# Hybrid encoder step: when the output GEMM's first operands, the last convolution and its edge rows are moved

## The reference

```python
u = jnp.concatenate([buf.astype(xin.dtype), cg * xin], axis=1)
y = sum(w[j] * u[:, j:j + S] for j in range(CONV_W))
return bg * y, u[:, S:]          # the two last rows of u are an output
...
y = jnp.concatenate([silu(z) * yb for yb, z in branches], axis=-1)
x = x + (y @ w_out)              # 2048 x 2048
...
y = x * rsqrt(mean(x * x) + eps) * g
```

## Time and profile before

| | us |
|---|---|
| median of 3 executions | 2401.81 |
| lowest, highest | 2400.15, 2405.1 |
| profiled execution, its own time | 2403.48 |
| its span in the trace | 2401.4 |
| PE busy | 2295.9 (96%) |
| DVE, ACT, POOL busy | 797.6, 481.9, 438.9 |

### The profile page before, as it was taken

The page is one execution under the profiler, slowest core; times in us unless marked ns, Lnnn a source line. Parts: engine busy times, 40 slices in busy tenths (PEclk is TensorE's granted clock), DMA queues, the critical chain, the costliest instruction groups (busy, mean ns, idle before and its releaser), DMA issues.

```text
span 2401.4 us, 35351 instructions
## 1 busy us (share of the span) xinstructions
PE 2295.9 (96%) x14176; PEld 2116.7 (88%) x14176; DVE 797.6 (33%) x1273; ACT 481.9 (20%) x798; POOL 438.9 (18%) x259
## 2 busy tenths in 40 slices
PE   6999999999989899999999999999899978999997
PEld 6899999999989899998999889999898976888886
DVE  7221122222121111153537361333231344343533
ACT  6111212222211111111111111111101013333431
POOL 2232221222121222222222122222121120000000
PEclk9999999999999999999999999999999988999999
DMA  5112414151431433231322223444434547465552
GB/s 213 56 58 68 182 44 168 55 174 51 161 112 56 150 125 124 107 96 53 114 71 95 84 69 117 126 125 126 99 108 163 197 139 263 155 224 185 187 194 87
DMA packets 158569, 298.90 MB, mean 124 GB/s; under 512 B 26124, under 2 KB 97932, under 8 KB 154656
## 3 DMA queue, kind: packets, MB, share of 16 engines
q1 hardware_dynamic: 150432, 281.63, 34.7%
q10 hardware_dynamic: 8064, 16.25, 2.1%
HBM read 238.55 MB, written 78.10 MB: 132 GB/s over the span
## 4 chain that ended last, share of the span: by engine, by line
PE 81%; DVE 9%; DMA 6%; issue 1%; SPq 1%; ACT 1%; DVEq 0%; POOLq 0%
PE G L820 18%; PE G L822 17%; PE G L821 17%; PE X L1161 3%; PE X L1160 3%; PE X L1159 3%; PE G L1159 3%; PE G L1160 3%; PE G L1161 3%; PE X L1030 2%; PE X L1009 1%; DMA conv_s<-cus 1%; PE X L1138 1%; PE X L919 1%; PE X L881 1%
## 5 line engine op out<-in xcount | busy, mean ns | idle before, releaser
L820 PE MATMUL G<-hhi,whi 128*128 128x384 f32 x2880 | 991.1, 344 | 7.2 <-POOL wlo L802 5.3
L822 PE MATMUL G<-hhi,wlo 128*128 128x384 f32 x2880 | 967.7, 336 | 0.0
L821 PE MATMUL G<-hlo,whi 128*128 128x384 f32 x2880 | 967.4, 336 | 0.0
L820 PEld LDWEIGHTS G<-hhi,whi 128*128 128x128 f32 x2880 | 544.4, 189 | 27.0 <-issue 11.3
L821 PEld LDWEIGHTS G<-hlo,whi 128*128 128x128 f32 x2880 | 544.5, 189 | 1.8
L822 PEld LDWEIGHTS G<-hhi,wlo 128*128 128x128 f32 x2880 | 543.4, 189 | 0.0
L800 POOL CAST whi<-wr 128x1024 fp32r<-128x1024 f32 x120 | 133.8, 1115 | 1491.2 <-PE G L822 1304.4
L802 POOL TENSOR_TENSOR wlo<-wr,whi 128x1024 fp32r<-128x1024 f32 x120 | 299.5, 2496 | 9.6
L1176 ACT ACTIVATE ev<-G 128x384 f32<-128x384 f32 x180 | 88.0, 490 | 669.7 <-PE G L822 669.5
L1908 DVE TENSOR_TENSOR olo<-orw,ohi 128x1024 fp32r<-128x1024 f32 x96 | 111.8, 1220 | 160.7 <-ACT ohi L1387 160.3
L1159 PE MATMUL G<-ohi,yhi 128*128 128x512 f32 x288 | 114.1, 396 | 20.5 <-DVE ylo L1902 20.5
(11 more groups left out here) (351 smaller groups left out, 1950.0 us busy)
## 6 DMA issues: line engine op xcount, KB each, us to landing
wr<-w_in_t SPq DMA_DIRECT2D x120, 512.0 KB, 5.2
orw<-w_out_t SPq DMA_DIRECT2D x96, 512.0 KB, 5.1
u_scratch<-ev SPq DMA_DIRECT2D x180, 192.0 KB, 1.9
xin<-x_all SPq DMA_DIRECT2D x9, 1024.0 KB, 4.9
cv<-u_scratch SPq DMA_DIRECT2D x16, 576.0 KB, 5.8
yr<-y_scratch SPq DMA_DIRECT2D x12, 768.0 KB, 8.2
xo<-x_all SPq DMA_DIRECT2D x3, 3072.0 KB, 12.7
y_all<-fo SPq DMA_DIRECT2D x9, 1024.0 KB, 4.1
```

The source lines that it names most:

```text
L820: mm(G[:, j, 0:GC], whi[:, kh, k], hhi[:, kk, hs], start=(kk == 0), stop=False)
L821: mm(G[:, j, 0:GC], whi[:, kh, k], hlo[:, kk, hs], start=False, stop=False)
L822: last = mm(G[:, j, 0:GC], wlo[:, kh, k], hhi[:, kk, hs], start=False, stop=(kk == 15))
```

## The change

- **SBUF layout.** `yhi`, `ylo` and `yr` are now lists of two halves; those for kh = 0 lie together over the first 8 blocks of `hhi`, those for kh = 1 over the last 8; `ohi[0]` and `olo[0]` lie over the first half of `hlo`, `ohi[1]` and `olo[1]` over the second.
- **Output GEMM's first operands.** SP loads y's quarters 0 and 1, and ACT and DVE split them and the first half of the weights, after PE is through half kh = 0 of tile 59 (`half0_mm`), not after all of tile 59. Quarters 2 and 3 follow when tile 59 is done and the first 384 columns of the fourth convolution have landed in `yT`.
- **Banks.** `outbank` gives X to even c and G to odd c. For c = 1, PE waits until tile 59's banks were copied.
- **Fourth convolution.** Tiles 58 and 59 are not stored to `uT`. ACT copies their banks straight to `cv[:, 2]`, tile 58's after the third convolution has read it, tile 59's after the fourth has. DVE's last product runs in three parts of 384 columns, placed among the output operands' splits.
- **Edges.** `conv_buf` is loaded once for all f into `cbuf`; DVE copies each f's part in, and the two last rows out into `cpo` and `cso`, which are stored by one DMA each at the end. The result alternates between `cv[:, 1]` and `cv[:, 0]`; SP no longer waits for stores before it loads cg, xin and z of the next, and bg is loaded one GEMM piece later.

```diff
-        yhi = sb(st7, "yhi", [128, KT, GC], R)
...
+        for kh in range(2):
+            yhi.append(sb(st7, f"yhi{kh}", [128, 8, GC], R))
+            ylo.append(sb(st7, f"ylo{kh}", [128, 8, GC], R))
+            yr.append(sb(st7, f"yr{kh}", [128, 2, 4, GC]))
...
         def outbank(c, a):
-            return G[:, a] if c % 2 == 0 else X[:, a]
+            return X[:, a] if c % 2 == 0 else G[:, a]
...
         def conv_in(eng, e, own, f):
-            eng.wait_ge(cv_in, 48 * f + 64)
+            if f < 3:
+                eng.wait_ge(cv_in, 32 * f + 64)
+            else:
+                eng.wait_ge(cv_in, 144)
+                eng.wait_ge(evac_done, 3 * T_CF(3, 0) + 6)
+            c = conv_y(f)
+            own(e.tensor_copy(cus[:, :, 0:2], cbuf[:, f]))
...
+            own(e.tensor_copy(cpo[:, f], cub[:, NP:NP + 2]))
+            own(e.tensor_copy(cso[:, f], cus[:, :, DT:DT + 2]))
...
             def store_conv(f):
                 sp.wait_ge(cv_done, f + 1)
-                sp.dma_start(yT[8 + f], cy).then_inc(cv_out, 16)
-                sp.dma_start(conv_p[f], cub[:, NP:NP + 2]).then_inc(cv_out, 16)
-                sp.dma_start(conv_s[f], cus[:, :, DT:DT + 2]).then_inc(cv_out, 16)
+                sp.dma_start(yT[8 + f], conv_y(f)).then_inc(cv_out, 16)
...
             for f in range(3):
-                pieces(CONV_AT + 5 * f, CONV_AT + 5 * f + 5)
+                if f:
+                    pieces(CONV_AT + 4 * f, CONV_AT + 4 * f + 1)
+                    load_conv_b(f)
+                    pieces(CONV_AT + 4 * f + 1, CONV_AT + 4 * f + 4)
+                else:
+                    pieces(CONV_AT, CONV_AT + 4)
                 store_conv(f)
-                sp.wait_ge(cv_out, 48 * f + 48)
                 load_conv(f + 1)
-                if f < 2:
-                    load_conv_b(f + 1)
-            pieces(CONV_AT + 15, LAST)
-            load_conv_b(3)
+            pieces(CONV_AT + 12, LAST)
+            sp.wait_ge(half0_mm, NTILES + 1)
+            for p in (0, 1):
+                load_y(0, p)
+            sp.wait_ge(cv_done, 4)
+            sp.dma_start(yT[11, :, 0:GC], conv_y(3)[:, 0:GC]).then_inc(cv_out, 16)
             sp.wait_ge(bank_full, 3 * NTILES + 3)
-            for p in (0, 1, 3):
-                load_y(0, p)
+            sp.wait_ge(cv_out, 64)
+            load_y(0, 2)
+            load_y(0, 3)
             load_out_w(0, 0, 1)
...
-            pieces(CONV_AT, LAST)
+            pieces(CONV_AT, LAST - 12)
+            def evac_conv(T, j, after):
+                act.wait_ge(bank_full, 3 * T + j + 4)
+                act.wait_ge(zero_done, after)
+                fn(cv[:, 2, GC * j:GC * j + GC], G[:, j, 0:GC], ACT.Copy).then_inc(evac_done, 1)
```

More of the change, by code:

```diff
@@ L237, in encoder_program @@
         st7 = ExitStack()
-        yhi = sb(st7, "yhi", [128, KT, GC], R)
[L239 to L242, removed]
+        yhi, ylo, yr, ohi, olo = [], [], [], [], []
+        for kh in range(2):
+            yhi.append(sb(st7, f"yhi{kh}", [128, 8, GC], R))
+            ylo.append(sb(st7, f"ylo{kh}", [128, 8, GC], R))
+            yr.append(sb(st7, f"yr{kh}", [128, 2, 4, GC]))
+        for kh in range(2):
+            ohi.append(sb(st7, f"ohi{kh}", [128, 8, 512], R))
+            olo.append(sb(st7, f"olo{kh}", [128, 8, 512], R))
+            if kh == 0:
+                sb(st7, "rest_of_hlo", [128, 1024])
         xo = sb(st7, "xo", [128, 3, D])
@@ L438, in store_u, with gemm @@
                 sp.dma_start(uT[T, :, GC * j:GC * j + GC], ev[:, j]).then_inc(u_stored[j], 16)
-            def gemm(T, kh, j, more=True):
+            def gemm(T, kh, j, more=True, store=True):
                 if j == 0 and more:
                     load_w(T + 1, kh)
-                if kh == 1:
+                if kh == 1 and store:
                     store_u(T, j)
@@ L1151, in _ @@
                             pe.wait_ge(ylo_done, 4 * t + 2 * kh + 6)
+                        if c == 1 and kh == 0:
+                            pe.wait_ge(evac_done, 3 * NTILES + 3)
                         for a in range(3):
@@ L1158, in _ @@
                                 ysl = slice(128 * a, 128 * a + 128)
-                                mm(o, yhi[:, kk, ysl], ohi[:, kh, k], start=(kk == 0), stop=False)
-                                mm(o, ylo[:, kk, ysl], ohi[:, kh, k], start=False, stop=False)
-                                last = mm(o, yhi[:, kk, ysl], olo[:, kh, k], start=False, stop=(kk == 15))
+                                mm(o, yhi[kh][:, k, ysl], ohi[kh][:, k], start=(kk == 0), stop=False)
+                                mm(o, ylo[kh][:, k, ysl], ohi[kh][:, k], start=False, stop=False)
+                                last = mm(o, yhi[kh][:, k, ysl], olo[kh][:, k], start=False, stop=(kk == 15))
                             if kh == 1:
@@ L1367, in _, with high_y @@
                     pieces(*glu_pieces(3 * f + j))
-            pieces(CONV_AT, LAST)
-            def high_y(t, kh):
-                for p in (2 * kh, 2 * kh + 1):
+            pieces(CONV_AT, LAST - 12)
[3 more added lines that the diff above has]
+                fn(cv[:, 2, GC * j:GC * j + GC], G[:, j, 0:GC], ACT.Copy).then_inc(evac_done, 1)
+            for j in range(3):
+                evac_conv(T_CF(3, 0), j, conv_read(2))
+            def high_y(t, ps):
+                for p in ps:
                     act.wait_ge(y_in[p], 16 * t + 16)
@@ L1391, in high @@
                     if c == 0:
-                        high_y(t, kh)
+                        high_y(t, (2 * kh, 2 * kh + 1))
                     high_w(t, c, kh)
+            act.wait_ge(half0_mm, NTILES + 1)
             high_w(0, 0, 0)
-            high_y(0, 0)
+            for j in range(3):
+                evac_conv(T_CF(3, 1), j, conv_read(3))
+                if j < 2:
+                    high_y(0, (j,))
+            high_y(0, (2, 3))
             high_w(0, 0, 1)
-            high_y(0, 1)
             for t in range(3):
@@ L1892, in _, with last_conv_b, low_y @@
                 conv_taps(v, own, f)
+                conv_z(dve, v, own, f)
                 if f < 3:
-                    conv_z(dve, v, own, f)
                     conv_b(v, f)
-            dve.wait_ge(bank_full, 3 * NTILES + 3)
-            def low_y(t, kh):
-                for p in (2 * kh, 2 * kh + 1):
+            def last_conv_b(j):
+                dve.wait_ge(evac_done, 3 * T_CF(3, 1) + j + 4)
+                conv_b(v, 3, slice(GC * j, GC * j + GC))
+            def low_y(t, ps):
+                for p in ps:
                     dve.wait_ge(yhi_done, 4 * t + p + 1)
-                    tt(ylo[:, 4 * p:4 * p + 4], yr[:, yslot(p)], yhi[:, 4 * p:4 * p + 4].bitcast(F), SUB).then_inc(ylo_done, 1)
+                    tt(ypart(ylo, p), yraw(p), ypart(yhi, p).bitcast(F), SUB).then_inc(ylo_done, 1)
             def low_w(t, c, kh):
@@ L1912, in low @@
                     if c == 0:
-                        low_y(t, kh)
+                        low_y(t, (2 * kh, 2 * kh + 1))
                     low_w(t, c, kh)
+            last_conv_b(0)
             low_w(0, 0, 0)
-            low_y(0, 0)
-            conv_z(dve, v, own, 3)
-            conv_b(v, 3)
+            low_y(0, (0, 1))
+            for j in (1, 2):
+                last_conv_b(j)
+            low_y(0, (2, 3))
             low_w(0, 0, 1)
-            low_y(0, 1)
             dve.wait_ge(g_loaded, 32)
```

67 lines of the change are left out of this document (42 added, 25 removed).

## The result

| | before | after |
|---|---|---|
| median, us | 2400.98 (4 executions) | 2372.03 (4) |
| lowest to highest | 2399.86 to 2405.1 | 2366.67 to 2375.31 |
| ratio | | 0.9874, 95% interval 0.985 to 0.9898 |
| profiled execution, its span | 2403.48, 2401.4 | 2366.67, 2364.9 |
| PE busy | 2295.9 | 2284.2 |

By the ratio the kernel is 1.26% faster; the forecast was 2370 us, range 2366 to 2378. The profiled execution after is the fastest of its four. Part of its lead comes from before the changed part: ACT's copy of tile 57's last bank lies at 1906.73, in the kernel before at 1912.44, and over all runs of this study at 1906.7 to 1915.1. So I compare from this copy to the start of the last matmul, which I call the stretch. It is 2386.97 - 1912.44 = 474.53 us before, and 2350.55 - 1906.73 = 443.82 after.

What follows compares the result with a forecast made beforehand. PE, busy 96% of the span, bounds the kernel. Gains of 7.89 + 16.7 + 7.5 = 32.1 to 32.2 us give 2371.3 from the profiled 2403.48, or 2369.6 from the median 2401.81; forecast 2370 us, range 2366 to 2378.

Steps and rivals of the forecast that it cites:

- Input tiles: Input GEMM's tiles 58 and 59: the 7.89 us lost to waits for `wlo` and the slower clock would go.
- The pause: PE's wait before its first output matmul: 17.74 us shrinks to 1 us, with DVE's order binding instead of y's loads.
- The chain: SP's loads and DVE's convolutions: convolution 3 ends at 1952.8, is wanted at 1954.6, with 1.8 us to spare.
- The row on the shared port: DVE beside POOL: each POOL half costs DVE 2.8 us, by the exclusive-lock rule up to 3.75 us.
- If there is no second pause: Output GEMM: first to last matmul takes 391.5 us, and the last starts at 2354.8, 32.2 us earlier.
- the rival of 25%: Output GEMM at c = 1: weights late, PE waits 2 to 4 us plus 1.7 for the clock; 2374, up to 2376; 25%.
- the order in a queue: DMA queue: descriptors are consumed in ring order, which speaks against putting more ahead of c = 1's weights.
- The reading of the profile before: Before the output GEMM: operands' splits come behind convolution 3, which SP's waits for stores delay; 17.74 us of PE idleness.

Runs made afterwards that it cites:

- pack_alone: The kernel before with packed edges alone (loaded once, stored once at the end, SP waits only for y's store); ratio 0.9936 to the kernel before.
- edge_wait: The changed kernel, but the first three convolutions store edge rows in 8-byte pieces and SP waits for them to land; ratio 0.9985 to the kernel before.
- edge_each: The changed kernel, but the first three convolutions each store their packed edge rows by two small DMAs, not waited for; ratio 0.9928 to the kernel before.
- dve_order: The changed kernel, but DVE makes the four first `olo` before the first third of the last product; ratio 0.9874 to the kernel before.
- conv3_delay: The changed kernel with four more DVE products (5.0 us in all, results unused) behind convolution 3's product with z; ratio 0.988 to the kernel before.
- after_again: The changed kernel unaltered, run once more on the chip of the last three runs; ratio 0.9868 to the kernel before.
- xo_late: The changed kernel, but `xo` and `go` load behind c = 1's first four weight quarters, DVE waiting for `go` only at the final norm; ratio 0.9872 to the kernel before.
- y_gate: The changed kernel, but y's first two quarters are loaded only when tile 59 is complete; ratio 0.9918 to the kernel before.

## Why the prediction was right

**Input tiles.** 7.89 us forecast, 7.89 measured. pack_alone shows that it needs only the packed edges and with them the shorter wait on SP; edge_wait and edge_each show that loss again (12.5 and 2.4 us of waits for `wlo`) when the chain gets long.

**The pause.** PE's start was forecast 9.28 us after tile 59's first bank copy; measured 1957.49 - 1948.33 = 9.16. That DVE's order binds there, as the step said, is shown by dve_order: with the four `olo` ahead, the pause is gone. The last product's third took 0.56 us (taken: 0.55).

**The chain.** Counted from tile 57's copy, convolutions 1, 2 and 3 were to end at 6.8, 25.7 and 40.4 us; they ended at 7.5, 26.3 and 39.8. In these three the small copies took 0.17 to 0.18 us each, 0.5 together (taken: 0.4). The load took 5.4 to 7.3 us with SP's issue (taken: 6.8). The slack was 2.4 us, forecast 1.8, and conv3_delay shows that it is the whole slack.

**The row on the shared port.** The tap of 128 columns again took 2.37 us beside POOL (1909.11) where the free one takes 0.35; convolutions 1 and 2 took 12.2 us from the first copy on, where convolution 3's instructions with a second product of 1.36 us come to 9.5. That is 2.7 us for each POOL half, near the 2.8 taken from rows. It is under the 3.75 us, the whole length of a POOL split, that the prediction worked out as the most that the exclusive lock of the Trainium skill (SBUF — State Buffer, section on the two separate sides) could cost.

**The term that was mis-sized.** "If there is no second pause" holds at the second half of c = 0, where quarter 2 landed in time. But the rival of 25%, that c = 1's weights are late, came true in its small form: 1.15 us of idle and 1.31 on the path in after, 0.54 in after_again. So the output stream took 393.06 us instead of the forecast 391.5, and the gain in the stretch is 30.7 us, not 32.2. The rival's higher price, 2 to 4 us and 1.7 for the clock, was too high: the clock stayed at 1.00. What the prediction said of the order in a queue is borne out by xo_late: with `xo` and `go` no longer ahead of them, these weights reach ACT 11.1 us earlier.

**The step that was wrong.** The reading of the profile before said that the operands' splits come behind convolution 3, as the reason of the 17.7 us. In pack_alone the convolution is done 9 us before tile 59, and 13.9 us of the pause are left. The pause was set by y's loads, behind tile 59's end and the store and reload of tile 59 in SP's queue (in y_gate, where no such store stands ahead of them, 10.0 us are left); the late chain, whose loads stood ahead of that store, added 3.8 us. The sum did not suffer: PE's start was worked out from the new order alone, and the change moves both causes. That the wrong reading cost nothing was luck in what was changed together; with the packing alone my reading would have had the pause under 9 us.

## What to carry to other kernels

When one engine issues all DMAs in order, price a store's landing wait by all that stands behind it, also what is not of its kind: here 7.5 to 9.1 us of waiting for the edge rows of each convolution to land cost 8 us through late input weights, and started the last stage later. In this kernel the small-piece stores were better kept out of the loop even when nobody waited for them (edge_each). And a pause has more than one cause queued up: move the first cause alone, and see what ends the wait then.

## What the runs showed of the hardware that was not expected

- Two small stores (1 KB and 8 KB) in the queue, not waited for, put the loads behind them 3.0 to 3.5 us later, 1.4 of it in SP's issue (0.43 and 0.90 us; a plain one takes 0.33).
- The issue of `xo` held SP for 4.79 us in after, where it began 4.7 us after the issue of y's quarters 2 and 3, and for 0.51 and 0.52 in edge_each and edge_wait, where it began 8.2 us after it; the same 3.7 MB were issued in between.
- PE's pauses of 0.9 and 1.15 us left the granted clock at 1.00, and so did the one of 2.01 us in dve_order. After the one of 2.76 us of the kernel before, 12 matmuls took 4.44 us instead of 2.72, and after that of 2.71 us in conv3_delay PEclk was 0.55.
- Two executions of one and the same program differ by up to 8.6 us (2366.67 to 2375.31), and the profiled executions of this study, whose work on PE is the same up to there, differ by 8.3 us already at tile 57's copy (1906.73 to 1915.05). A change of 2 us can be seen in the trace of such a kernel, but hardly in its time.
